# A hybrid RWKV/MoE step on one core: expert weights in six 2 MB units, gather by a stationary selection, biases in 32-row quadrants

## The chip, the core and the metric

One core of a Trainium2 chip runs the whole kernel in one launch. Times are device microseconds of that core. The engines are TensorE (PE, its weight loads are shown apart as PEld), VectorE (DVE), ScalarE (ACT), GpSimd (POOL) and SyncE (SP), which here only issues transfers. Transfers run on the core's 16 DMA engines. The metric is the time of one execution, as the median of several runs.

## The reference, cut to what matters

Two streams of 128 tokens (context and latent, D = 1024) go through one layer: modulation, norm, an input projection, a pooling and an RWKV branch, an output projection, and then a mixture of 32 experts, each token with the 4 experts that its router picks. The change touches the experts alone. All weights and activations are f32.

```python
def moe(h, lp):
    xt = h.reshape(B * T, D)
    logits = (xt @ lp['router_w'] + lp['router_b']).astype(jnp.float32)
    top_v, top_i = lax.top_k(logits, TOP_K)
    top_w = jax.nn.softmax(top_v, axis=-1)
    combine = jnp.sum(jax.nn.one_hot(top_i, N_EXPERTS, dtype=jnp.float32) * top_w[..., None], axis=1)
    for e in range(N_EXPERTS):
        gu = xt @ lp['expert_w_gu'][e] + lp['expert_b_gu'][e]
        glu = jnp.minimum(gu[:, :D_FF], SWIGLU_LIMIT)
        lin = jnp.clip(gu[:, D_FF:], -SWIGLU_LIMIT, SWIGLU_LIMIT)
        act = glu * jax.nn.sigmoid(SWIGLU_ALPHA * glu) * (lin + 1.0)
        out = out + combine[:, e:e + 1] * (act @ lp['expert_w_down'][e] + lp['expert_b_down'][e])
```

An expert's weights are 1024 x 2048 (gate and up, 8 MB) and 1024 x 1024 (down, 4 MB).

## The kernel before, in words

The first 390 us do everything up to the router. Then a loop runs over work items. An item is one expert with up to 64 of its tokens (SLOTS); an expert with more tokens gets further items. With these inputs there are 32 items. Every engine has its own loop over the items, and semaphores tie them together; the order within an engine is the order of the code.

**Weights.** `ring` holds 12 slots of 1 MB (128 partitions of 8 KB), one item's weights. SyncE (`expert_chunk`, L380 to L388, loop at L418) waits until `chunk_used` says that a slot has been read, and issues the same slot of the next item. Slots 0 to 7 hold gate and up, slot j the rows 128 j to 128 j + 127 (8 KB a partition, one run). Slots 8 to 11 hold down, two blocks of 128 rows each (two runs of 4 KB a partition).

**TensorE, one item** (L1185 to L1233). The stationary operand is always the small one, 64 slots wide, the moving operand is 512 columns of weights. Two output halves `h` go to the two 64-partition halves of a bank, so two 64-column tiles of the array work side by side. In turn:
- gate and up (L1192): 8 chunks by 4 matmuls into banks G (gate) and L (up). After chunk 1 the gate's bias is added (L1175, `up_bias(G, 0, False)`): the stationary `sele` has row e set to ones and picks row e of the bias table.
- `gather()` for the next item (L1147): 16 matmuls, x in 128-column blocks stationary, the 0/1 selection `p2` (64 columns) moving. It leaves the chosen tokens already transposed, hidden dimension on partitions; ScalarE copies them to `xg` (L1521).
- four transposes of the activation (L1203), two of the weighted selection (L1208).
- down (L1216): 4 chunks by 4 matmuls into G, with the down bias (L1222) after the first chunk.
- the up bias of the next item into L (L1175, `up_bias(L, FF, True)`).
- scatter (L1232): the result times the weighted selection, added into banks 0 to 3, in two row tiles of 64.

**VectorE, one item:** the weighted selection (L1973), the next selection (L1903), then after gate and up: clip the gate (L1981), clip the up part (L1982), (up + 1) times gate (L1984), times the sigmoid (L1987), the copy of the transposed activation (L1989), and the next `sele` (L1907). **ScalarE:** the sigmoid with its table load (L1532), the copy of the gathered tokens (L1521), of the transposed selection (L1535), of the down result (L1538).

**GpSimd** fills the unused rows of the bias tables with zeros ahead of the loop and loads them.

## Time and profile before

| | us |
|---|---|
| median of 3 runs | 1373.55 |
| lowest, highest | 1370.78, 1376.55 |
| the profiled execution | 1377.59 |
| its span, first to last instruction | 1375.8 |
| TensorE busy | 1315.5 |
| VectorE busy | 342.0 |
| ScalarE busy | 201.3 |
| GpSimd busy | 34.5 |
| mean granted clock | 0.98 |

The profile is that of one execution. The span is 1.8 us shorter than the time of the same execution. "Granted clock" is the share of TensorE's full 2.4 GHz. "PEld" rows are the weight loads, which run ahead of the matmuls that they belong to; since their starts are recorded and the ends of matmuls are modelled, the prediction reads distances between starts of loads. An f32 matmul is recorded as two loads and two matmuls.

### The profile page before, as it was taken

How to read it: one execution, taken by the hardware profiler on the slowest of the kernel's cores; microseconds unless marked ns; L12 is line 12 of the kernel's file. 1: busy time of each engine (PE TensorE's matmuls, PEld its weight loads, DVE VectorE, ACT ScalarE, POOL GpSimd, SP SyncE). 2: the span in 40 equal slices, each digit the busy share in tenths (PEclk: the TensorE clock that was granted, in tenths of full speed). 3: DMA queues.
4: the chain of work that ended last, by engine and by line, in shares of the span. 5: the costliest groups of instructions: out<-in, count | busy, mean ns of one | idle time of the engine just before them, and what ended most of it. 6: DMA issues, size and time to landing. Idle time of an engine off the chain costs nothing.

```text
span 1375.8 us, 19277 instructions
## 1 busy us (share of the span) xinstructions
PE 1315.5 (96%) x7509; PEld 687.7 (50%) x7509; DVE 342.0 (25%) x756; ACT 201.3 (15%) x365; POOL 34.5 (3%) x72
## 2 busy tenths in 40 slices
PE   4999999999999999999999999999999999999996
PEld 2676789878744344444443444444344444444442
DVE  0558962304331111111111111111111112111113
ACT  2331123110221111111111111111111111111111
POOL 3000110010000000000000000000000000000000
PEclk8899999979999999999999999999999999999998
DMA  9968401247459999999999999999999999999990
GB/s 325 330 208 301 135 12 53 93 157 288 171 232 402 416 414 408 415 415 415 413 413 408 412 415 412 413 416 407 415 413 409 415 415 416 413 405 414 416 385 30
DMA packets 109388, 462.45 MB, mean 336 GB/s; under 512 B 10695, under 2 KB 33902, under 8 KB 76558
## 3 DMA queue, kind: packets, MB, share of 16 engines
q1 hardware_dynamic: 107134, 457.68, 84.1%
q0 software_dynamic: 848, 3.03, 0.6%
q10 hardware_dynamic: 1376, 1.31, 0.3%
q8 instruction: 22, 0.36, 0.1%
q14 instruction: 8, 0.07, 0.0%
HBM read 460.66 MB, written 1.33 MB: 336 GB/s over the span
## 4 chain that ended last, share of the span: by engine, by line
PE 92%; DVE 4%; DMA 2%; issue 1%; SPq 1%; ACT 0%; DVEq 0%
PE bank L1192 32%; PE bank L1216 16%; PE bank L1147 9%; PE bank L1232 4%; PE bank L1175 4%; PE bank L608 4%; PE bank L633 3%; PE bank L1044 2%; PE bank L1081 2%; PE bank L1222 2%; DMA ring<-in_w_mod 2%; DVE pmT L1989 2%; PE bank L1203 1%; PE bank L564 1%; PE bank L744 1%; PE bank L946 1%
## 5 line engine op out<-in xcount | busy, mean ns | idle before, releaser
L1192 PE MATMUL bank<-ring,gate 128*64 128x512 f32 x2048 | 451.9, 594 | 0.0
L1192 PEld LDWEIGHTS bank<-ring,gate 128*64 128x64 f32 x2048 | 144.3, 137 | 298.2 <-issue 298.1
L1216 PE MATMUL bank<-ring,pmT 128*64 128x512 f32 x1024 | 232.4, 595 | 20.5 <-DVE pmT L1989 20.5
L1981 DVE TENSOR_SCALAR gate<-bank 128x512 f32<-128x512 f32 x32 | 22.1, 692 | 563.5 <-PE bank L1192 563.5
L1216 PEld LDWEIGHTS bank<-ring,pmT 128*64 128x64 f32 x1024 | 73.1, 137 | 153.6 <-issue 153.6
L1147 PEld LDWEIGHTS bank<-vt,bt 128*128 128x128 f32 x1024 | 116.7, 192 | 26.0 <-issue 26.0
L1147 PE MATMUL bank<-vt,bt 128*128 128x64 f32 x1024 | 121.1, 276 | 0.0
L1532 ACT ACTIVATE corr<-gate 128x512 f32<-128x512 f32 x32 | 20.1, 630 | 521.6 <-DVE gate L1981 521.6
L1175 PE MATMUL bank<-qr,vt 128*64 128x512 f32 x260 | 67.0, 592 | 0.0
L1232 PE MATMUL bank<-kk 64*128 64x512 f32 x256 | 63.6, 615 | 0.0
L633 PE MATMUL bank<-hnT,ring 128*128 128x256 f32 x240 | 56.6, 392 | 2.9 <-issue 2.9
L1538 ACT ACTIVATE kk<-bank 128x512 f32<-128x512 f32 x32 | 19.1, 597 | 262.6 <-PE bank L1216 262.6
L608 PE MATMUL bank<-hnT,ring 128*128 128x256 f32 x256 | 55.9, 379 | 0.0
L633 PEld LDWEIGHTS bank<-hnT,ring 128*128 128x128 f32 x240 | 45.8, 195 | 14.0 <-issue 7.9
L608 PEld LDWEIGHTS bank<-hnT,ring 128*128 128x128 f32 x256 | 48.5, 190 | 6.5
L1907 DVE COPY vt<-ident 128x64 f32 (+1 forms) x33 | 6.5, 196 | 152.7 <-PE bank L1216 152.7
L1232 PEld LDWEIGHTS bank<-kk 64*128 64x128 f32 x256 | 22.0, 186 | 41.0 <-issue 41.0
L1532 ACT ACT_TABLE_LOAD x32 | 41.1, 1283 | 1.9 <-DVE tick L1964 1.3
L1175 PEld LDWEIGHTS bank<-qr,vt 128*64 128x64 f32 x260 | 18.9, 137 | 37.0 <-issue 37.0
L564 PE MATMUL bank<-ring,cpad 128*32 128x256 f32 x384 | 29.5, 441 | 7.8 <-DMA ring<-in_w_mod 7.8
L1989 DVE COPY pmT<-bank 128x512 f32<-128x512 f32 x32 | 22.1, 692 | 45.1 <-PE bank L1203 45.1
L1222 PE MATMUL bank<-qr,vt 128*64 128x512 f32 x128 | 33.1, 592 | 0.0
(352 smaller groups left out, 975.4 us busy)
## 6 DMA issues: line engine op xcount, KB each, us to landing
ring<-in_expert_w_gu SPq DMA_DIRECT2D x256, 1024.0 KB, 8.6
ring<-in_expert_w_down SPq DMA_DIRECT2D x128, 1024.0 KB, 7.6
ring<-in_w_mod SPq DMA_DIRECT2D x24, 1024.0 KB, 10.4
ring<-in_w_in SPq DMA_DIRECT2D x17, 1024.0 KB, 8.1
ring<-in_w_o SPq DMA_DIRECT2D x4, 1024.0 KB, 9.7
ring<-in_w_pool_out SPq DMA_DIRECT2D x2, 1024.0 KB, 7.0
ring<-in_w_rwkv_out SPq DMA_DIRECT2D x2, 1024.0 KB, 11.8
pr<-gate_rows POOLq DMA_DIRECT2D x4, 512.0 KB, 7.3
```

What stands on the lines that cost most here:

```text
L564: last = mm(out[32 * j:32 * (j + 1), :], cpad[:, 2 * r + k, :], w[:, k, j * MW:(j + 1) * MW], start=(r + k == 0), stop=(r == MC - 1 and k ...
L608: last = mm(o, ring_in(c)[:, k, (m % 2) * P:(m % 2 + 1) * P], hnT[:, k, :], start=(k == 0), stop=(k == KT - 1))
L633: last = mm(banks[n % 2][:, 0:TT], w[:, k, o:o + P], hnT[:, k, :], start=(i == 0), stop=(i == KT - 1))
L1044: last = mm(banks[m % 4][:, 0:TT], ring_in(c)[:, k, (m % 4) * P:(m % 4 + 1) * P], src[:, k, :], start=(k == 0), stop=(k == 3))
L1147: last = mm(banks[6][:, k * SLOTS:(k + 1) * SLOTS], x2t[:, s, k * P:(k + 1) * P], p2[:, s, 0:SLOTS], start=(s == 0), stop=(s == NS - 1))
L1175: mm(b[h * SLOTS:(h + 1) * SLOTS, :], sele, bgu[:, o + h * 512:o + (h + 1) * 512], start=start, stop=False)
L1192: last = mm(b[h * SLOTS:(h + 1) * SLOTS, :], xg[:, j, :], ring[:, j, o + h * 512:o + (h + 1) * 512], start=(j == 0 and b is G), stop=(j == ...
L1216: last = mm(G[h * SLOTS:(h + 1) * SLOTS, :], actT[:, c % 4, c // 4, :], ring[:, GU_CHUNKS + j, i * D + h * 512:i * D + (h + 1) * 512], sta ...
L1222: mm(G[h * SLOTS:(h + 1) * SLOTS, :], sele, bdn[:, h * 512:(h + 1) * 512], start=False, stop=False)
L1232: last = mm(banks[2 * s + h][:, :], pwt[r, s, :], ysb[r, :], start=False, stop=True, skip_group_check=True)
L1532: af(sgb, gsb, ACT.Sigmoid, scale=ALPHA).then_inc(S("sg_ready"), 1)
L1989: v.tensor_copy(actT.rearrange("p j h s -> p (j h s)"), banks[5][:, :]).then_inc(S("actT_ready"), 1)
```

## The change

- **Weights:** six units of 2 MB instead of twelve of 1 MB. A unit takes two neighbouring slots. Partition p gets the rows 2p and 2p + 1 of a block of 256 (gate and up), or rows 4p to 4p + 3 of a block of 512 (down), one run of 16 KB. The first item's units are issued a little later, when two slots are free at once.
- **Gather:** the selection is stationary (64 columns), x is moving (512 columns): 4 matmuls, in the middle of gate and up, with the tokens on partitions. ScalarE copies the result to `xgt`, TensorE turns it in four transposes with a stride of 2 (`gather_turn`), and ScalarE copies that to `xg`.
- **Activation transposes:** they read `act_[:, i::4]`, a stride of 4, to match the new order of the down rows.
- **Biases:** the table of 2048 gate-and-up biases is laid out as four groups of 32 partitions (one for each 512 columns), the down table as two groups. `sele` has row e of every quadrant set (`quad`), and each bias matmul reads 32 rows. All four gate and up biases come after scatter, the two down biases after the gate has been evicted and ahead of the activation's transposes. GpSimd no longer fills the tables.

```diff
-    bgu = area[:, 0:2048]
-    bdn = area[:, 2048:3072]
+    bgu = area[:, 0:512]
+    bdn = area[0:2 * NE, 512:1024]
...
+        def expert_unit(e, u):
+
+            if u < GU_UNITS:
+                src = A["expert_w_gu"][0][bass.ds(e, 1), 2 * P * u:2 * P * (u + 1), :].rearrange("o (p i) n -> p (o i n)", i=2)
             else:
...
+                r = 4 * P * (u - GU_UNITS)
+                src = A["expert_w_down"][0][bass.ds(e, 1), r:r + 4 * P, :].rearrange("o (p i) n -> p (o i n)", i=4)
+            sp.dma_start(ring[:, 2 * u:2 * u + 2, :].rearrange("p g n -> p (g n)"), src).then_inc(S(f"slot{2 * u}_full"), 16)
...
         def gather():
-            for k in range(KT):
-                for s in range(NS):
-                    last = mm(banks[6][:, k * SLOTS:(k + 1) * SLOTS], x2t[:, s, k * P:(k + 1) * P], p2[:, s, 0:SLOTS],
+
+            for s in range(NS):
+                for h in range(2):
+                    last = mm(banks[6][h * SLOTS:(h + 1) * SLOTS, :], p2[:, s, 0:SLOTS], x2t[:, s, h * 512:(h + 1) * 512],
                               start=(s == 0), stop=(s == NS - 1))
             last.then_inc(S("gathered"), 1)
+
+        def gather_turn():
+
+            for jj in range(2):
+                for i in range(2):
+                    c = 2 * jj + i
+                    last = tr(banks[6][:, c * P:(c + 1) * P], xgt[:, 2 * P * jj + i:2 * P * (jj + 1):2], ident[:])
+            last.then_inc(S("xgT_done"), 1)
...
+        def up_bias():
+
+            for b, r in ((G, 0), (L, 2)):
+                for h in range(2):
+                    q = slice((r + h) * NE, (r + h + 1) * NE)
+                    mm(b[h * SLOTS:(h + 1) * SLOTS, :], sele[q, :], bgu[q, :], start=True, stop=False)
...
+                if u == 1:
+                    pe.wait_ge(S("sel_ready"), it + 2)
+                    gather()
+
+            pe.wait_ge(S("xgt_ready"), it + 2)
+            gather_turn()
             pe.wait_ge(S("pw_ready"), it + 1)
...
+            pe.wait_ge(S("g_ready"), it + 1)
+            for h in range(2):
+                q = slice(h * NE, (h + 1) * NE)
+                last = mm(G[h * SLOTS:(h + 1) * SLOTS, :], sele[q, :], bdn[q, :], start=True, stop=False)
+            last.then_inc(S("sele_used"), 1)
+
+            pe.wait_ge(S("act_ready"), it + 1)
+            for i in range(4):
+                last = tr(L[:, i * P:(i + 1) * P], act_[:, i::4], ident[:])
+            last.then_inc(S("actT_done"), 1)
...
+            pe.wait_ge(S("sele_ready"), it + 2)
+            up_bias()
```

TensorE in the loop of the kernel before, from the last gate-and-up chunk to the first down chunk; `pmT` is the activation, `vt` the selections, `qr` the bias tables:

```order
L1192 MATMUL bank<-ring,gate 64x512 [waits slot7_full]
L1198 REGISTER_ALU
L1147 MATMUL bank<-vt,bt 128x64 [waits sel_ready]
L1147 MATMUL bank<-vt,bt 128x64 x15
L1203 MATMUL bank<-ident,pmT 128x128 [waits act_ready]
L1203 MATMUL bank<-ident,pmT 128x128 x3
L1208 MATMUL bank<-ident,vt 128x128 [waits pw_ready]
L1212 REGISTER_ALU [waits actT_ready]
L1216 MATMUL bank<-ring,pmT 64x512 [waits slot8_full]
```

The same place after the change; `raw` holds the gathered tokens ahead of their transposes:

```order
L1200 MATMUL bank<-ring,gate 64x512 [waits slot6_full]
L1200 MATMUL bank<-ring,gate 64x512 x7
L1155 MATMUL bank<-ident,raw 128x128 [waits xgt_ready]
L1155 MATMUL bank<-ident,raw 128x128 x3
L1211 MATMUL bank<-ident,vt 128x128 [waits pw_ready]
L1217 MATMUL bank<-qr,vt 64x512 [waits g_ready]
L1222 MATMUL bank<-ident,pmT 128x128 [waits act_ready]
L1222 MATMUL bank<-ident,pmT 128x128 x3
L1228 REGISTER_ALU [waits actT_ready]
L1232 MATMUL bank<-ring,pmT 64x512 [waits slot8_full]
```

The 16 gather matmuls are gone from here; four transposes and the down bias stand ahead of the activation's transposes.

TensorE at the end of an item, before:

```order
L1216 MATMUL bank<-ring,pmT 64x512 [waits slot11_full]
L1216 MATMUL bank<-ring,pmT 64x512 x3
L1175 MATMUL bank<-qr,vt 64x512 [waits sele_ready]
L1175 MATMUL bank<-qr,vt 64x512
L1232 MATMUL bank<-kk 128x512 [waits ysb_ready,pwt_ready]
L1232 MATMUL bank<-kk 128x512 x3
```

And after:

```order
L1232 MATMUL bank<-ring,pmT 64x512 [waits slot10_full]
L1232 MATMUL bank<-ring,pmT 64x512 x7
L1241 MATMUL bank<-kk 128x512 [waits ysb_ready,pwt_ready]
L1241 MATMUL bank<-kk 128x512 x3
L1183 MATMUL bank<-qr,vt 64x512 [waits sele_ready]
L1183 MATMUL bank<-qr,vt 64x512 x3
```

The bias matmuls moved from ahead of scatter to behind it, and are four instead of two.

## Rows read from the trace of the kernel before

**Rows 1.** The page, busy time by engine, and the chain that ended last
```profile
PE 1315.5 (96%) x7509; PEld 687.7 (50%) x7509; DVE 342.0 (25%) x756; ACT 201.3 (15%) x365; POOL 34.5 (3%) x72
...
PE 92%; DVE 4%; DMA 2%; issue 1%; SPq 1%; ACT 0%; DVEq 0%
```

**Rows 2.** Stretches of one item, then the last item whole: busy us, granted clock, DMA
```profile
core 0: us, PE busy (x) PEld busy (x) DVE busy (x) ACT busy (x) POOL busy (x), PEclk, DMA share, GB/s
907.88:922.62 14.74, 14.74 (x71) 4.79 (x69) 0.00 (x0) 0.00 (x0) 0.00 (x0) 1.00 1.02 420
922.62:927.70 5.08, 4.45 (x40) 4.21 (x38) 3.37 (x5) 1.61 (x3) 0.00 (x0) 1.00 1.00 418
927.70:936.44 8.74, 8.73 (x40) 2.88 (x40) 1.28 (x5) 0.72 (x2) 0.00 (x0) 1.00 1.01 412
936.44:938.36 1.92, 1.92 (x10) 0.69 (x9) 0.00 (x0) 1.16 (x1) 0.00 (x0) 1.00 1.01 382
...
1334.65:1365.13 30.48, 29.84 (x156) 12.56 (x154) 4.21 (x8) 2.21 (x4) 0.00 (x0) 1.00 0.15 60
```

**Rows 3.** The page, costliest groups: busy us, mean ns, the bias matmuls
```profile
L1175 PE MATMUL bank<-qr,vt 128*64 128x512 f32 x260 | 67.0, 592 | 0.0
```

**Rows 4.** Timeline of the same item: start us, us, engine, line, [idle before]
```profile
908.36 0.14 PEld L1192 LDWEIGHTS bank<-ring,gate 128*64 128x64 f32 x2 [0.28 <-issue]
...
921.66 0.14 PEld L1192 LDWEIGHTS bank<-ring,gate 128*64 128x64 f32 x2 [0.28 <-issue]
922.62 3.65 PEld L1147 LDWEIGHTS bank<-vt,bt 128*128 128x128 f32 x32 [0.81 <-issue]
...
922.74 0.69 DVE L1981 TENSOR_SCALAR gate<-bank 128x512 f32<-128x512 f32 x1 [17.79 <-PE bank L1192]
...
923.46 0.63 ACT L1532 ACTIVATE corr<-gate 128x512 f32<-128x512 f32 x1 [16.35 <-DVE gate L1981]
...
924.79 0.69 DVE L1987 TENSOR_TENSOR pmT<-corr 128x512 f32<-128x512 f32 x1
926.13 0.48 PEld L1203 LDWEIGHTS bank<-ident,pmT 128*128 128x128 f32 x4
...
927.70 0.20 PEld L1216 LDWEIGHTS bank<-ring,pmT 128*64 128x64 f32 x4 [0.87 <-issue]
```

**Rows 5.** Timeline, the end of the same item and the next one's start
```profile
934.62 0.15 PEld L1216 LDWEIGHTS bank<-ring,pmT 128*64 128x64 f32 x2 [0.28 <-issue]
...
935.70 0.60 ACT L1538 ACTIVATE kk<-bank 128x512 f32<-128x512 f32 x1 [8.21 <-PE bank L1216]
936.31 1.28 ACT L1532 ACT_TABLE_LOAD   x1
936.44 0.30 PEld L1232 LDWEIGHTS bank<-kk 64*128 64x128 f32 x4 [0.81 <-issue]
...
938.36 0.20 PEld L1192 LDWEIGHTS bank<-ring,gate 128*64 128x64 f32 x4 [0.76 <-issue]
```

**Rows 6.** Timeline early on: modulation matmuls in four 32-column tiles, and what follows
```profile
58.65 0.59 PEld L564 LDWEIGHTS bank<-ring,cpad 128*32 128x32 f32 x16 [0.76 <-issue]
...
59.65 0.51 PEld L633 LDWEIGHTS bank<-hnT,ring 128*128 128x128 f32 x3 [0.41 <-issue]
```

**Rows 7.** Issues of one item (timeline), landing of the first and the eighth (by line)
```profile
910.00 13.20 SPq L388 DMA_DIRECT2D ring<-in_expert_w_gu  x8
...
DMA to landing us min/median/max: 6.5/6.5/6.5
...
DMA to landing us min/median/max: 11.1/11.1/11.1
```

**Rows 8.** Stretches around two falls of the granted clock, columns as in rows 2
```profile
265.20:268.50 3.30, 3.30 (x22) 2.50 (x18) 2.54 (x5) 0.00 (x0) 0.00 (x0) 1.00 1.05 406
268.60:285.50 16.90, 16.90 (x59) 14.07 (x59) 0.00 (x0) 1.32 (x4) 0.00 (x0) 0.50 0.26 96
43.30:46.50 3.20, 3.20 (x9) 2.52 (x8) 1.59 (x3) 0.00 (x0) 0.00 (x0) 0.50 1.06 378
```

More of the change, by code:

```diff
@@ L419, in _ @@
             e = sp.value_load(item[0:1, bass.ds(it, 1)], min_val=0, max_val=NE - 1)
[L420 to L423 removed]
+            for u in range(NU):
+                sp.wait_ge(S("chunk_used"), it * NU + (u + 1 - NU))
+                expert_unit(e, u)
         sp.wait_ge(S("stored"), 96)
@@ L1159, in _ @@
         pe.wait_ge(S("sel_ready"), 1)
-        for k in range(KT):
-            for s in range(NS):
-                last = mm(banks[6 + k // 4][:, (k % 4) * P:(k % 4 + 1) * P], x2t[:, s, k * P:(k + 1) * P], p2[:, s, :],
-                          start=(s == 0), stop=(s == NS - 1))
-        last.then_inc(S("gathered"), 1)
+        gather()
         pe.wait_ge(S("e16_ready"), 1)
@@ L1180, in _ @@
+        pe.wait_ge(S("bgu_in"), 64)
+        pe.wait_ge(S("bdn_in"), 32)
         pe.wait_ge(S("sele_ready"), 1)
-        up_bias(L, FF, True)
         pe.wait_ge(S("items_ready"), 1)
         n_items = pe.value_load(item[0:1, ITEMS:ITEMS + 1], min_val=NE, max_val=NE + EXTRA)
+        up_bias()
         with pe.Fori(0, n_items) as it:
             pe.wait_ge(S("xg_ready"), it + 1)
-            for j in range(GU_CHUNKS):
-                pe.wait_ge(S(f"slot{j}_full"), it * 16 + 16 * (FRONT_USES[j] + 1))
-                for b, o in ((G, 0), (L, FF)):
-                    for h in range(2):
-                        last = mm(b[h * SLOTS:(h + 1) * SLOTS, :], xg[:, j, :], ring[:, j, o + h * 512:o + (h + 1) * 512],
-                                  start=(j == 0 and b is G), stop=(j == GU_CHUNKS - 1))
-                last.then_inc(S("chunk_used"), 1)
-                if j == 1:
-                    up_bias(G, 0, False)
-            pe.wait_ge(S("sel_ready"), it + 2)
-            gather()
-            pe.wait_ge(S("act_ready"), it + 1)
-            for j in range(4):
-                last = tr(L[:, j * P:(j + 1) * P], act_[:, j * P:(j + 1) * P], ident[:])
-            last.then_inc(S("actT_done"), 1)
@@ new lines, in _ @@
+            for u in range(GU_UNITS):
+                pe.wait_ge(S(f"slot{2 * u}_full"), it * 16 + 16 * (FRONT_USES[2 * u] + 1))
+                w = ring[:, 2 * u:2 * u + 2, :]
+                for i in range(2):
+                    for b, o in ((G, 0), (L, FF)):
+                        for h in range(2):
+                            last = mm(b[h * SLOTS:(h + 1) * SLOTS, :], xg[:, 2 * (u % 2) + i, u // 2, :], w[:, i, o + h * 512:o + (h + 1) * 512],
+                                      start=False, stop=(u == GU_UNITS - 1 and i == 1))
+                last.then_inc(S("chunk_used"), 1)
+                if u == 1:
+                    pe.wait_ge(S("sel_ready"), it + 2)
+                    gather()
@@ L1520, in gathered_out, with gather_turn_out @@
             act.wait_ge(S("gathered"), n)
-            af(xg.rearrange("p k s -> p (k s)"), banks[6][:, :], ACT.Copy).then_inc(S("xg_ready"), 1)
-        act.wait_ge(S("gathered"), 1)
-        for j in range(2):
-            last = af(xg[:, 4 * j:4 * j + 4, :], banks[6 + j][:].rearrange("p (k s) -> p k s", k=4)[:, :, 0:SLOTS], ACT.Copy)
-        last.then_inc(S("xg_ready"), 1)
+            af(xgt, banks[6][:, :], ACT.Copy).then_inc(S("xgt_ready"), 1)
+        def gather_turn_out(n):
+            act.wait_ge(S("xgT_done"), n)
+            af(xg.rearrange("p k h s -> p (k h s)"), banks[6][:, :], ACT.Copy).then_inc(S("xg_ready"), 1)
+        gathered_out(1)
+        gather_turn_out(1)
         act.wait_ge(S("items_ready"), 1)
```

92 lines of the change are left out of this document (39 added, 53 removed).

## The prediction

> **What bounds the kernel now.** The shares of the span and the chain of work come first [rows 1]: TensorE is busy for 96% and holds 92% of the chain, transfers 2%. The reader should then ask what TensorE waits for, and read the table by stretches for one expert (an item) [rows 2]. An item takes 30.48 us: 14.74 gate and up, 5.08 until the down weights start, 8.74 down, 1.92 scatter. The granted clock is 1.00 in all four stretches, so the full 2.4 GHz.
>
> The same rows show a second resource that is full: the 16 DMA engines' share is 1.00 to 1.02, at 382 to 420 GB/s. Which of the two sets the pace? The last item, the last of these rows, has nearly no transfers beside it (share 0.15) and also takes 30.48. And of the eight gate-and-up issues of an item the first, at 910.0, landed after 6.5 us and the last, at 922.9 (910.00 + 13.20 less its own 0.33), after 11.1 [rows 7], where a slot is used again a round of 30.48 after its last use, so some 28 us after the issue. Their landings are (922.9 + 11.1 - 910.0 - 6.5) / 7 = 2.50 us apart, so 12 MB need 30.0 us. TensorE sets the pace, with the transfers 1 to 2% behind. Larger units can thus give nothing by themselves; what decides is how TensorE's own item changes.
>
> **The unit of the sum.** Within a stretch the weight loads come in pairs (two 64-column tiles side by side, each row of the view is a pair), 31 intervals from 908.36 to 921.66 [rows 4]: 0.429 us a step. Every f32 matmul is two instructions, so a pair of 512-column matmuls takes two steps. Scatter has 4 steps and takes 1.92 [rows 5], so a change of tiling costs about 0.20 on top.
>
> **Part by part, per item.**
> 1. Gate and up. Today 34 steps: 32 for the weights, 2 for the gate bias. The bias leaves (-2), the new gather with the selection stationary comes in between units 1 and 2: 4 matmuls of 512 columns, 64-column tiles in pairs, 4 steps. No tiling changes. +0.86.
> 2. From the last up matmul to the first down load, 5.08 today. The old gather (32 instructions) holds TensorE from 922.62 to 926.13, 3.51; the activation chain on VectorE is done before that, at 924.79 + 0.69 = 925.48 [rows 4], 2.86 into the stretch. With the gather gone, the chain ends last. What TensorE does meanwhile is hidden: six transposes of 0.11 each (the four loads of L1203 take 0.48 with a last one of 0.14), 0.7 us together, then the down bias, which waits for the gate's eviction (922.74 + 0.69, 0.81 in) and takes two steps and a change of tiling, so it is over near 2.0. The activation's transposes start at 2.86 + 0.06 for the hand-over, then the same 1.57 (926.13 to 927.70) as today. 4.49, -0.59. On ScalarE the copy of the gathered rows and a second table load (1.28 us [rows 5]) come ahead of the sigmoid, in its wait of 16.35 us for the gate [rows 4]; the copy of the turned rows comes behind it, beside VectorE's three remaining operations. They cost nothing while that wait stays above some 2 us.
> 3. Down. The two bias steps inside go: -0.86. The up bias at its end (two steps, half of L1175's 8 instructions per item [rows 3]) lay in the wait for ScalarE's copy of the result: last down load 934.62, copy 935.70 to 936.30, scatter 936.44 [rows 5]. Taking it out frees at most the 0.14 behind the copy; I take 0.05. -0.91.
> 4. After scatter comes a new, exposed piece: all four up biases, 32 rows by 64 columns each, in four quadrants. If the four run at once: 2 steps and a change of tiling, 0.86 + 0.20. The nearest row for four at once is L564, 16 instructions of 256 columns from 58.65 to 59.65 [rows 6]: 4 steps of 0.215 and 0.14. Bounds 0.9 (if the change of tiling is 0.04) and 1.92 (only two at once, as scatter); I take 1.04, near L564. Behind it waits the next item's first weight matmul, and nothing covers it.
>
> Sum: +0.86 - 0.59 - 0.91 + 1.04 = +0.40 us an item, 30.9. The last item's bias is behind its scatter and ends nothing: 31 x 0.40 - 0.64 = +11.8. Ahead of the loop the first gather shrinks, but it then needs a copy, transposes and a copy, beside VectorE's list of items; the four biases come after the register load. I put that at 0, give or take 1. GpSimd's dropped fills, its bias transfers in six parts instead of two, and VectorE's one new reduction early on lie beside longer work of TensorE, and the first experts' units are issued during the output projection, over 15 us ahead of their use; these go at nothing.
>
> **The clock.** It fell to 0.50 after 265.2 to 268.5, though TensorE shows busy for all 3.30 us [rows 8]; these are pairs of 64-column matmuls with a change of tiling after each, so few columns flow. It held in today's 5.08 [rows 2]. The new 4.5 us stretch is emptier: 0.7 of transposes, 0.9 of bias, about 0.9 of waiting, 0.45 of transposes, 1.1 of waiting. It lies between these rows. A short fall costs about half of 3.2 us (the stretch from 43.3 to 46.5) [rows 8], 1.6. I count two falls in 32 items, +3.2, and keep none and ten for the range.
>
> **Transfers.** An item of 30.9 leaves them 0.9 us of room. With 2 MB units a slot comes free later, but each still has over 20 us until its use. SyncE issues 6 per item instead of 12 and has nothing else in its queue in the loop.
>
> Forecast: +11.8 + 3.2 = +15.0. The profiled execution took 1377.59 (span 1375.8 and 1.8 around it) and would become 1392.6; it is 4 above the median of the runs, 1373.55, so the predicted median is 1388.6, rounded to 1389.
>
> **What the Trainium skill says.** L564's row shows four tiles at once at nearly full gain. The page "TensorE: Matmul & The Clock Gate", Part 3, gives a measured 3.07x for four 32-row tiles at 512 columns; by it the quadrants' 0.86 would be 1.12, and the time 8 us more. The page on SBUF ("SBUF — State Buffer", the note on cachelines) says that reads which cross to a new 16-byte line each time pay a penalty, and names 4 fp32 as the limit of a free stride; the activation's new transposes read with a stride of 4 floats, those of the gather with 2. No row here has such a read. That rule is rival B.
>
> **Rivals.**
> A. Only two quadrant tiles at once: the biases cost 1.92, +0.88 x 31 = +27, and 1373.6 + 11.8 + 27 = 1413, with no falls of the clock since the new stretch is filled longer. For it: scatter with its two row tiles runs in pairs. Against: L564's four.
> B. Strided reads slow the four exposed transposes. Doubled, 4 x 0.11 = 0.44 an item: +14: 1403. For the gather's transposes it would be hidden.
> C. The clock falls in ten items, not two: +16 instead of +3: 1401. It is decided by how the emptier stretch counts, which only the new clock rows can show.
> D. The transfers become the bound. They start to hold TensorE when 12 MB take over 31.5 us (31 rounds of 30.9, and some 18 us of slack that the full ring gives), 2.62 per MB against 2.50. At 2.72: 31 x 32.6 - 31 x 30.9 - 18 = +35: 1424. Nothing here shows 16 KB runs, but 8 KB and 4 KB runs land alike.
> E. Faster: the quadrant biases slip into the drain of the scatter and cost nothing exposed. 31 x (0.40 - 1.04) = -20: 1353. It decides below 0.64. Against: scatter is itself followed by a gap before the next load (0.76 idle behind L1232 [rows 5]).
> F. No measurable change: several terms each a tenth smaller, the clock holding: +5: 1379.
>
> **How the numbers follow.** Forecast 47% (1381 to 1396), A 12%, B 12%, C 13%, D 3%, E 4%, F 9%. The range 1379 to 1414 takes in the forecast, A, B, C and F's upper edge, some 83%. A measurement of this kernel can tell 0.5%, 6.9 us, from no change. Faster by more is E, 4%; within it F and a sliver of the forecast, 10%; slower 86%.
>
> **What would show it.** Right: the item is 30.8 to 31.0; gate and up 15.6; the stretch after it 4.5 with a wait on VectorE's product before the activation's transposes; scatter start to next item 2.9 to 3.0; the DMA share drops below 1.0. Wrong: the quadrant matmuls start in pairs 0.43 apart (A); the activation's transposes are spaced 0.2 (B); the mean granted clock of the loop falls below 0.99 (C); TensorE waits for a slot (D); the next item's first load follows the scatter by under 0.6 (E).

## The result and the profile after

| | before | after |
|---|---|---|
| median of the runs, us | 1373.8 | 1394.9 |
| lowest, highest | 1370.8, 1376.6 | 1393.7, 1395.4 |
| the profiled execution | 1377.59 | 1394.64 |
| its span | 1375.8 | 1392.9 |
| first gate-and-up load of the loop | 389.54 | 386.68 |
| one item (start of gate and up to the next) | 30.48 | 30.93, four of them 32.62 |

The ratio is 1.0153, 95% interval 1.0130 to 1.0175: slower by 21 us, where 15 were forecast. From the start of the loop to the end of the span it is 986.3 us before and 1006.2 after, +19.9. That sum closes: without the falls the 31 items are 13.7 longer (0.44 each), four falls of the clock by 1.70 are 6.8, and the last item with what follows is 0.5 shorter, as it has no bias behind it.

The page of the changed kernel: busy time, the chain that ended last, and from the costliest groups those in which TensorE now waits and the new bias matmuls. Columns as in [rows 1] and [rows 3].

```profile
PE 1268.3 (91%) x6853; PEld 596.7 (43%) x6853; DVE 340.8 (24%) x757; ACT 254.9 (18%) x429; POOL 31.1 (2%) x74
...
PE 84%; DVE 10%; ACT 2%; DMA 2%; issue 2%; SPq 1%; DVEq 0%
...
L1232 PE MATMUL bank<-ring,pmT 128*64 128x512 f32 x1024 | 233.6, 610 | 27.5 <-DVE pmT L2006 27.5
...
L1241 PE MATMUL bank<-kk 64*128 64x512 f32 x256 | 63.6, 611 | 25.1 <-ACT kk L1554 25.1
...
L1222 PE MATMUL bank<-ident,pmT 128*128 128x128 f32 x128 | 23.9, 310 | 30.3 <-DVE pmT L2004 30.3
...
L1183 PE MATMUL bank<-qr,vt 32*64 32x512 f32 x264 | 35.9, 613 | 0.8 <-issue 0.8
```

In the profiled executions TensorE is busy for 47 us less and the kernel takes 17 us longer: work was taken out of places where it filled a wait, and put where nothing covers it. VectorE's part of the chain rose from 4% [rows 1] to 10%. TensorE now stands still at three places in each item: 0.95 us for VectorE's product ahead of the activation's transposes, 0.86 for its copy of them, 0.78 for ScalarE's copy of the down result. Before, it stood still at one of them, 0.64 for the copy of the transposes, as the waits of the kernel before show (engine, line, what it waited for: us in total, times, longest):

```profile
PE bank L1216 <- DVE pmT L1989: 20.5, 32, 0.6
```

The table by stretches of one item (915.86 to 946.78), to be read against [rows 2], then the 850 us in the middle of the loop:

```profile
core 0: us, PE busy (x) PEld busy (x) DVE busy (x) ACT busy (x) POOL busy (x), PEclk, DMA share, GB/s
915.86:931.46 15.60, 15.60 (x77) 5.08 (x73) 0.00 (x0) 1.88 (x2) 0.00 (x0) 1.00 0.98 400
931.46:935.98 4.52, 2.71 (x17) 1.48 (x15) 3.47 (x6) 1.39 (x3) 0.00 (x0) 1.00 1.01 431
935.98:943.82 7.84, 7.08 (x32) 2.28 (x33) 1.08 (x4) 0.70 (x2) 0.00 (x0) 1.00 1.00 405
943.82:946.78 2.96, 2.93 (x16) 0.98 (x16) 0.00 (x0) 1.19 (x1) 0.00 (x0) 1.00 1.01 426
...
450.00:1300.00 850.00, 780.06 (x3668) 269.83 (x3666) 122.85 (x270) 140.93 (x191) 0.00 (x0) 0.99 0.99 404
```

Gate and up +0.86, the stretch ahead of down -0.56, down -0.90, scatter and biases +1.04. In the two long stretches the transfers moved 420 and 412 GB/s before [rows 2] and move 400 and 405 here, and their share stays at 0.98 to 1.00: it doesn't show that they are the limit.

The timeline around the two new places, to be read against [rows 4] and [rows 5]:

```profile
933.62 0.69 DVE L2004 TENSOR_TENSOR pmT<-corr 128x512 f32<-128x512 f32 x1
934.37 0.56 PEld L1222 LDWEIGHTS bank<-ident,pmT 128*128 128x128 f32 x4 [1.83 <-DVE pmT L2004]
...
935.97 0.20 PEld L1232 LDWEIGHTS bank<-ring,pmT 128*64 128x64 f32 x4 [1.05 <-issue]
...
943.82 0.33 PEld L1241 LDWEIGHTS bank<-kk 64*128 64x128 f32 x4 [1.64 <-issue]
...
945.76 0.21 PEld L1183 LDWEIGHTS bank<-qr,vt 32*64 32x64 f32 x8 [0.76 <-issue]
...
946.78 0.65 PE L1200 MATMUL bank<-ring,gate 128*64 128x512 f32 x2
```

VectorE's product ends at 934.31, and the transposes' loads begin at 934.37: the activation chain ends last, as forecast. The eight loads of the four bias matmuls stand within 0.21 us, and the next weight matmul follows 1.02 after the first of them: two pairs, one after the other, would need four steps of 0.43, so all four quadrants ran at once.

### The profile page after: what moved, and what is told of

Same layout as the page of the kernel before. It is cut to its first block, busy times and chain, and to the rows that moved or that the text cites. A ratio compares the mean times of both kernels' runs of the same rounds, so it can differ in the third digit from the quotient of the medians.

```text
span 1392.9 us, 17218 instructions
## 1 busy us (share of the span) xinstructions
PE 1268.3 (91%) x6853; PEld 596.7 (43%) x6853; DVE 340.8 (24%) x757; ACT 254.9 (18%) x429; POOL 31.1 (2%) x74
## 4 chain that ended last, share of the span: by engine, by line
PE 84%; DVE 10%; ACT 2%; DMA 2%; issue 2%; SPq 1%; DVEq 0%
PE bank L1200 32%; PE bank L1232 17%; PE bank L1241 5%; PE bank L606 4%; PE bank L1146 4%; PE bank L631 3%; PE bank L1183 2%; PE bank L1042 2%; PE bank L1079 2%; PE bank L1222 2%; DVE corr L2001 2%; DVE pmT L2006 2%; DVE pmT L2004 2%; DMA ring<-in_w_mod 2%; DVE gate L1998 2%
## 5 line engine op out<-in xcount | busy, mean ns | idle before, releaser
L1533 ACT ACTIVATE raw<-bank 128x512 f32<-128x512 f32 x33 | 19.7, 597 | 340.8 <-PE bank L1146 340.8
L1146 PE MATMUL bank<-bt,vt 128*64 128x512 f32 x264 | 62.3, 592 | 0.0
L1241 PEld LDWEIGHTS bank<-kk 64*128 64x128 f32 x256 | 24.8, 186 | 65.6 <-issue 65.6
L1222 PE MATMUL bank<-ident,pmT 128*128 128x128 f32 x128 | 23.9, 310 | 30.3 <-DVE pmT L2004 30.3
L1222 PEld LDWEIGHTS bank<-ident,pmT 128*128 128x128 f32 x128 | 17.9, 209 | 58.5 <-DVE pmT L2004 58.5
L1183 PE MATMUL bank<-qr,vt 32*64 32x512 f32 x264 | 35.9, 613 | 0.8 <-issue 0.8
L1146 PEld LDWEIGHTS bank<-bt,vt 128*64 128x64 f32 x264 | 18.9, 137 | 37.1 <-issue 37.1
```

Of the source, the lines that this page charges most:

```text
L1146: last = mm(banks[6][h * SLOTS:(h + 1) * SLOTS, :], p2[:, s, 0:SLOTS], x2t[:, s, h * 512:(h + 1) * 512], start=(s == 0), stop=(s == NS - 1))
L1183: mm(b[h * SLOTS:(h + 1) * SLOTS, :], sele[q, :], bgu[q, :], start=True, stop=False)
L1222: last = tr(L[:, i * P:(i + 1) * P], act_[:, i::4], ident[:])
L1241: last = mm(banks[2 * s + h][:, :], pwt[r, s, :], ysb[r, :], start=False, stop=True, skip_group_check=True)
L1533: af(xgt, banks[6][:, :], ACT.Copy).then_inc(S("xgt_ready"), 1)
```

## The experiments

All ran on the chip, with the kernel before beside them (medians 1372.5 to 1374.0). "Item" is the distance from one item's first gate-and-up load to the next's. Items and falls of the clock are those of the one profiled execution of each kernel; e6_gather_blocks and e7_plain_turns ran once, and their time is that one execution's.

### One part at a time

**e1_units: the kernel before with the 2 MB units alone.**

```diff
-            for j in range(RING):
-                sp.wait_ge(S("chunk_used"), it * RING + (j + 1 - RING))
-                expert_chunk(e, j)
+            for u in range(NU):
+                sp.wait_ge(S("chunk_used"), it * NU + (u + 1 - NU))
+                expert_unit(e, u)
...
-                    last = mm(banks[6][:, k * SLOTS:(k + 1) * SLOTS], x2t[:, s, k * P:(k + 1) * P], p2[:, s, 0:SLOTS],
+                        last = mm(banks[6][:, k * SLOTS:(k + 1) * SLOTS], x2t[:, s, 2 * P * u + i:2 * P * (u + 1):2], p2[:, s, 0:SLOTS],
...
-                last = tr(L[:, j * P:(j + 1) * P], act_[:, j * P:(j + 1) * P], ident[:])
+                last = tr(L[:, i * P:(i + 1) * P], act_[:, i::4], ident[:])
```

> The kernel before with the 2 MB units alone: six issues per item, 16 KB runs, x read with a stride of 2 by the old gather, the activation's transposes with a stride of 4; old gather, old bias tables and old places. Main theory (units are free, TensorE's own item decides): item 30.48 us as before, gate and up 14.74, the stretch after it 5.08, no falls of the clock in the loop, 1371 to 1377 us, ratio 1.000. Rival U (the 2 MB units carry the loss): the whole difference of 17 to 21 us shows here, 1390 or more, with waits for a slot. Rival S (strided reads): 16 strided stationary loads and 4 strided transposes lengthen the 5.08 to over 5.3, and the time to over 1381.

Measured: 1381.1 us, ratio 1.0049 (1.0031 to 1.0066). Item 30.75, no fall of the clock in the loop, no wait for a slot. The main theory missed: the units aren't free. Rival S holds. The timeline of e1_units, weight loads behind gate and up:

```profile
922.64 3.85 PEld L1147 LDWEIGHTS bank<-vt,bt 128*128 128x128 f32 x32 [0.81 <-issue]
926.35 0.60 PEld L1198 LDWEIGHTS bank<-ident,pmT 128*128 128x128 f32 x4
926.86 0.26 PEld L1203 LDWEIGHTS bank<-ident,vt 128*128 128x128 f32 x2
927.99 0.20 PEld L1213 LDWEIGHTS bank<-ring,pmT 128*64 128x64 f32 x4 [0.87 <-issue]
```

From the first gather load to the first transpose it is 3.71 us against 3.51 in [rows 4], and the whole stretch takes 5.35 against 5.08.

**e6_gather_blocks: e1_units with x in blocks of neighbouring columns.**

```diff
-                        last = mm(banks[6][:, k * SLOTS:(k + 1) * SLOTS], x2t[:, s, 2 * P * u + i:2 * P * (u + 1):2], p2[:, s, 0:SLOTS],
+                        last = mm(banks[6][:, k * SLOTS:(k + 1) * SLOTS], x2t[:, s, k * P:(k + 1) * P], p2[:, s, 0:SLOTS],
```

> The kernel before with the 2 MB units alone, as e1_units, but x read by the old gather in blocks of 128 neighbouring columns; the weights' rows then meet the wrong hidden rows, so this computes something else. e1_units had an item of 30.75 against 30.48, its 32 gather loads spread over 3.71 us against 3.51 and the transposes' four over 0.51 against 0.45. Theory (the stride of the reads is all that the units cost): 0.20 comes back, item 30.54 to 30.56. Rival (the larger transfers disturb TensorE's reads): 30.75.

Measured: 1374.9 in one run, item 30.55, and in its timeline 3.51 us again from the gather to the transposes:

```profile
918.85 3.65 PEld L1147 LDWEIGHTS bank<-vt,bt 128*128 128x128 f32 x32 [0.81 <-issue]
922.36 0.59 PEld L1198 LDWEIGHTS bank<-ident,pmT 128*128 128x128 f32 x4
```

So the transfers themselves cost TensorE nothing. The row order of the larger unit does, where it makes a stationary load read with a stride: 0.20 us for 32 loads with a stride of two floats, 0.07 for the four loads with a stride of four.

**e2_old_gather: the changed kernel with the old gather.**

```diff
-                if u == 1:
-                    pe.wait_ge(S("sel_ready"), it + 2)
-                    gather()
-
-            pe.wait_ge(S("xgt_ready"), it + 2)
-            gather_turn()
+            pe.wait_ge(S("sel_ready"), it + 2)
+            gather()
```

> The changed kernel with the old gather: x stationary, 16 matmuls of 64 columns behind gate and up, no turn of the gathered rows; the order behind it is activation transposes, selection transposes, down bias. Main theory: gate and up 13.88, then 5.08 plus up to 0.4 since the down bias (0.9 to 1.06) is longer than the rest of the wait for the activation's copy, down 7.84, scatter and biases 2.96: item 30.0 to 30.2, and no falls of the clock (3.5 us of matmuls stand in that stretch): 1358 to 1366 us. The transfers, 2.50 us per MB, then end at 30.0 and may set it. Rival (the new gather is not what costs, the quadrant biases are): item 30.9 and more, 1388 or more.

Measured: 1368.7, ratio 0.9956 (0.9941 to 0.9972), item 30.34, no fall in the loop. Gate and up 13.89, the next stretch 5.65, down 7.85, scatter and biases 2.96. The item is 0.14 over the upper end of the expectation, for which the stride's price in the gather, 0.20, is enough (not known when it was written): from the first gather load to the first transpose it is 3.70 here. The time is 3 us over its upper end. This is faster than both kernels: with the new gather taken out, the changed kernel gains. The rival (the exposed quadrant biases cost) is out.

**e3_old_bias: the changed kernel with the old biases.**

```diff
+                if u == 0:
+                    up_bias(G, 0, False)
...
-            for h in range(2):
-                q = slice(h * NE, (h + 1) * NE)
-                last = mm(G[h * SLOTS:(h + 1) * SLOTS, :], sele[q, :], bdn[q, :], start=True, stop=False)
-            last.then_inc(S("sele_used"), 1)
...
+                    if u == 0 and i == 1:
+                        for h in range(2):
+                            last = mm(G[h * SLOTS:(h + 1) * SLOTS, :], sele, bdn[:, h * 512:(h + 1) * 512], start=False, stop=False)
...
+            up_bias(L, FF, True)
             pe.wait_ge(S("pwt_ready"), it + 1)
             pe.wait_ge(S("ysb_ready"), it + 1)
...
-            up_bias()
```

> The changed kernel with the old biases: full-height tables, the gate's bias between units 0 and 1, the down bias inside down, the up bias ahead of scatter; the gather is the new one. Main theory: gate and up 16.46, the next stretch 4.5, down 8.7, scatter 1.92: item 31.6, +0.67 against the changed kernel, 1415 us with its four falls of the clock. With the down bias gone from the stretch ahead of down, that stretch is emptier still: if it is its emptiness that makes the clock fall, there are more than four falls of 1.7 us, up to one in nearly each item, 1415 to 1455. Rival (falls come from something else, as the transfers): four or fewer, 1408 to 1416. Rival for the biases (the exposed quadrants cost more than they save): below 1395.

Measured: 1444.0, ratio 1.0504. An undisturbed item takes 31.64, +0.71 against the changed kernel, as expected. 18 of 31 items have a fall of the clock. One of them, from the item's start to the fall, and the 3.4 us behind it (columns as in the table above); then TensorE's timeline ahead of that fall:

```profile
452.76:474.40 21.64, 18.83 (x92) 7.01 (x92) 3.37 (x5) 3.27 (x5) 0.00 (x0) 1.00 0.99 411
474.40:477.80 3.40, 3.40 (x10) 1.01 (x8) 0.00 (x0) 0.00 (x0) 0.00 (x0) 0.50 1.00 424
```

```profile
469.81 0.38 PE L1211 MATMUL bank<-ident,vt 128*128 128x128 f32 x2
472.14 0.75 PE L1216 MATMUL bank<-ident,pmT 128*128 128x128 f32 x4 [1.95 <-DVE pmT L2001]
473.75 3.06 PE L1226 MATMUL bank<-ring,pmT 128*64 128x512 f32 x8 [0.86 <-DVE pmT L2003]
```

Ahead of the fall TensorE had waited 1.95 and 0.86 us with four transposes between. With the down bias out of this stretch the falls went from 4 items to 18: that speaks for the emptiness of this stretch and against the transfers (their share is 0.99 here too); e10_both_fillers tests it from the other side.

The four corners, item in us without falls (2 MB units in all):

| | old biases | new biases |
|---|---|---|
| old gather | 30.75 | 30.34 |
| new gather | 31.64 | 30.93 |

The new biases gain 0.41 or 0.71, the new gather costs 0.89 or 0.59, and only the two kernels with it have falls in the loop. So the item's way from 30.48 to 30.93 is +0.27 for the units, +0.59 for the gather and -0.41 for the biases, added in the order units, biases, gather.

### The falls of the clock

**e4_filler: one more matmul in the wait for VectorE's product.**

```diff
             pe.wait_ge(S("g_ready"), it + 1)
+            mm(G[:, 0:256], ident[:], xgt[:, 0:256], start=True, stop=True)
             for h in range(2):
```

> The changed kernel with one more matmul (the identity stationary, 256 columns of the gathered rows moving, into the gate's bank ahead of the down bias, which overwrites it), in VectorE's stretch where TensorE waits. It adds 0.43 us of work that ends at about 2.4 of 2.9 us. Main theory: item 30.93 unchanged, the four falls of the clock in the loop vanish, 4 x 1.7 = 6.8 us less, 1388. Rival: the falls have nothing to do with how full this stretch is: 1395, falls as many. Second rival: the work is not hidden: +0.4 x 31 = 13 more.

Measured: 1392.6, item 30.93, three falls instead of four. Hidden it was, but it didn't do what was expected. The falls stand just behind the stretch (685.0, with the first down load at 684.5), so the next run puts the matmul later.

**e5_filler_late: the same matmul behind the activation's transposes.**

```diff
             last.then_inc(S("actT_done"), 1)
 
+            pe.wait_ge(S("xg_ready"), it + 2)
+            mm(banks[6][:, 0:256], ident[:], xgt[:, 0:256], start=True, stop=True)
+
             pe.wait_ge(S("actT_ready"), it + 1)
```

> The changed kernel with one more matmul of 256 columns (0.43 us), this time behind the activation's transposes, in the wait of 1.1 us for VectorE's copy of them. With the same matmul ahead of the down bias three falls of the clock in the loop were left of four, each just behind this place (685.0, 934.1, 1183.3, where the activation's transposes and the wait are over at 684.5). Theory: it is the part from the activation's transposes to the first down loads that is too empty: no fall in the loop, item 30.93, 1388 us. Rival: work anywhere in the stretch does not matter, three or four falls stay: 1393 to 1395. Second rival: it delays the first down load: +0.1 to 0.4 an item, 3 to 12 us more.

Measured: 1392.1, item 30.93, three falls again. The theory that the late part alone decides fell. Three against four says little by itself: e7_plain_turns below, with no filling at all, has two. A stretch of e5_filler_late ahead of a fall and the 3.5 us behind it; TensorE is busy for 5.1 of 6.5 us, and yet the clock goes to half:

```profile
710.00:716.50 6.50, 5.13 (x28) 2.30 (x26) 3.46 (x6) 1.39 (x3) 0.00 (x0) 1.00 1.03 441
716.50:720.00 3.50, 3.50 (x10) 1.00 (x8) 1.09 (x4) 0.00 (x0) 0.00 (x0) 0.51 1.00 426
```

**e10_both_fillers: both places, the second with 384 columns.**

```diff
             pe.wait_ge(S("g_ready"), it + 1)
+            mm(G[:, 0:256], ident[:], xgt[:, 0:256], start=True, stop=True)
...
+            pe.wait_ge(S("xg_ready"), it + 2)
+            mm(banks[6][:, 0:384], ident[:], xgt[:, 0:384], start=True, stop=True)
```

> The changed kernel with extra matmuls at both places: 256 columns ahead of the down bias (0.43 us) and 384 columns behind the activation's transposes (0.64 us, in the wait of 1.1). Either place alone left three falls of four. Theory (the stretch between the last up and the first down load is too empty as a whole, and a fall comes when enough of the emptiness falls together): no fall in the loop, item 30.93, 1386 to 1389 us. Rival (the falls come from something that a fuller stretch does not change): three or four falls, 1391 to 1395. Second rival: the work delays the first down load: +0.1 to 0.3 an item, 3 to 9 us more.

Measured: 1387.7, ratio 1.0103 (1.0086 to 1.0120), all 31 items at 30.93, no fall. The middle of the loop, with the row of the changed kernel above at 0.99:

```profile
450.00:1300.00 850.00, 813.77 (x3798) 284.31 (x3796) 122.77 (x270) 140.87 (x191) 0.00 (x0) 1.00 1.00 407
```

7.1 us less than the changed kernel, for four falls of 1.70. More work for TensorE, less time. That the emptiness of the stretch brings the falls is shown from both sides: emptier, 18 items with a fall; filled at both places, none. Filling one place leaves three. How full the stretch has to be is not shown.

### The strided transposes

**e7_plain_turns: the changed kernel, both sets of transposes on neighbouring columns.**

```diff
-                    last = tr(banks[6][:, c * P:(c + 1) * P], xgt[:, 2 * P * jj + i:2 * P * (jj + 1):2], ident[:])
+                    last = tr(banks[6][:, c * P:(c + 1) * P], xgt[:, c * P:(c + 1) * P], ident[:])
...
-                last = tr(L[:, i * P:(i + 1) * P], act_[:, i::4], ident[:])
+                last = tr(L[:, i * P:(i + 1) * P], act_[:, i * P:(i + 1) * P], ident[:])
```

> The changed kernel with both sets of transposes reading neighbouring columns (the gathered rows and the activation); the hidden rows then meet the wrong weights, so this computes something else. The four loads of the activation's transposes took 0.56 us against 0.48 before. Theory (a stride of 4 costs a little): the four back at 0.48, item 30.85 to 30.88, 2 us less. Rival (the 0.05 by which the item missed the forecast lies elsewhere): item 30.93.

Measured: one run of 1387.0, with two falls; item 30.83, 0.10 less. From the lines of 500 to 1300 us, the activation's transposes: first this kernel, then the changed one.

```profile
L1222 PEld LDWEIGHTS bank<-ident,pmT 128*128 128x128 f32 x100 | 10.4, 140 | 46.4 <-DVE pmT L2004 46.4
```

```profile
L1222 PEld LDWEIGHTS bank<-ident,pmT 128*128 128x128 f32 x100 | 14.0, 209 | 45.7 <-DVE pmT L2004 45.7
```

A load with a stride of four floats takes 209 ns against 140; from the first of these loads to the first down load it is 1.51 us here and 1.60 in the changed kernel. That is the whole 0.10 of the item, 3 us in all; the gathered rows' transposes, made plain too, give nothing, as they lie in a wait.

### Where the room is, and what the transfers allow

**e8_packed_units: old gather and quadrant biases, each in a wait.** The gather is split around the activation's transposes, the selection's transposes go into the gate's bank, and the down result into bank 7, so that the gate's and up's banks are free when ScalarE copies the result. The four biases then run in that wait.

```diff
             pe.wait_ge(S("sel_ready"), it + 2)
-            gather()
+            gather(0)
             pe.wait_ge(S("act_ready"), it + 1)
...
             last.then_inc(S("actT_done"), 1)
 
+            gather(1)
             pe.wait_ge(S("pw_ready"), it + 1)
...
-                last = tr(banks[7][:, s * T:(s + 1) * T], pw[:, s, :], ident[:])
+                last = tr(G[:, s * T:(s + 1) * T], pw[:, s, :], ident[:])
...
-                        last = mm(G[h * SLOTS:(h + 1) * SLOTS, :], actT[:, i, u, :], w[:, i, h * 512:(h + 1) * 512],
+                        last = mm(banks[7][h * SLOTS:(h + 1) * SLOTS, :], actT[:, i, u, :], w[:, i, h * 512:(h + 1) * 512],
...
             pe.wait_ge(S("pwt_ready"), it + 1)
+            pe.wait_ge(S("sele_ready"), it + 2)
+            up_bias()
+
             pe.wait_ge(S("ysb_ready"), it + 1)
```

> The old gather (strided x) split around the activation's transposes, 12 matmuls ahead and 4 behind; selection transposes into the gate's bank; down result and down bias in the bank 7, so that gate's and up's banks are free early and all four quadrant biases run in the wait for ScalarE's copy of the result; 2 MB units. TensorE's own item by the rows of the run with the old gather: 30.34 - 1.04 for the biases + 0.2 to 0.3 of change of tiling = 29.5. Main theory: the transfers then set the pace (2.50 us per MB in the profile of before): item 30.0 to 30.1, TensorE waits for slots, 1356 to 1361 us. Rival: transfers can go faster when they are asked to, item 29.5, 1343. Rival: 2 MB units are slower than 1 MB (landings at 404 GB/s): item 30.3 and more, no gain over 1368.7.

Measured: 1344.6, ratio 0.9790 (0.9773 to 0.9807), item 29.55 throughout. The rival that the transfers can go faster is right: no wait for a slot. The end of an item in its timeline:

```profile
944.56 0.21 PEld L1172 LDWEIGHTS bank<-qr,vt 32*64 32x64 f32 x8 [0.81 <-issue]
944.56 1.09 PE L1172 MATMUL bank<-qr,vt 32*64 32x512 f32 x8
944.68 0.60 ACT L1533 ACTIVATE kk<-bank 128x512 f32<-128x512 f32 x1 [7.38 <-PE bank L1218]
945.29 1.28 ACT L1527 ACT_TABLE_LOAD   x1
945.58 0.30 PEld L1230 LDWEIGHTS bank<-kk 64*128 64x128 f32 x4 [0.81 <-ACT kk L1533]
```

The biases run beside ScalarE's copy (944.68 to 945.28), and scatter begins at 945.58, 0.30 behind the copy. The piece of 1.04 us behind scatter has become 0.2: from the last down load to scatter it is 1.97 us, against 1.78 in e2_old_gather. Splitting the gather gives nothing: from gate and up to the first down load it is 5.71, against 5.64.

**e9_packed_chunks: the same order with twelve transfers of 1 MB and plain reads.**

```diff
-            for u in range(NU):
-                sp.wait_ge(S("chunk_used"), it * NU + (u + 1 - NU))
-                expert_unit(e, u)
+            for j in range(RING):
+                sp.wait_ge(S("chunk_used"), it * RING + (j + 1 - RING))
+                expert_chunk(e, j)
...
-                last = tr(L[:, i * P:(i + 1) * P], act_[:, i::4], ident[:])
+                last = tr(L[:, i * P:(i + 1) * P], act_[:, i * P:(i + 1) * P], ident[:])
```

> The same order of TensorE's work with the old 1 MB transfers, twelve per item, and plain x blocks and transposes. TensorE's own item: 29.5 - 0.27 = 29.2. Main theory (transfers set the pace, the size of a transfer does not matter): the same item as the run with 2 MB units within 0.05 us, 30.0 to 30.1, 1356 to 1361 us. Rival (size matters): the two differ by over 0.1 us an item. Rival (TensorE still sets it): this one is 0.27 an item faster, 1335 to 1350.

Measured: 1347.2, ratio 0.9810 (0.9790 to 0.9831). The item is 29.41 for 23 items, then 30.12: the ring's slack is used and TensorE waits for slots. The main theory, that the size of a transfer doesn't matter, missed. TensorE's own item is 0.14 under that of e8_packed_units, not 0.27: behind the split gather only the strided loads from the transposes on are exposed. The waits of e9_packed_chunks (engine, line, what it waited for: us in total, times, longest), and its middle in the table by stretches; below them the same row of e8_packed_units:

```profile
PE bank L1194 <- DMA ring<-in_expert_w_gu: 4.4, 9, 0.5
```

```profile
450.00:1300.00 850.00, 845.43 (x4428) 345.71 (x4426) 134.64 (x290) 96.21 (x143) 0.00 (x0) 1.00 1.02 418
```

```profile
450.00:1300.00 850.00, 850.00 (x4438) 355.26 (x4434) 134.62 (x290) 96.92 (x145) 0.00 (x0) 1.00 1.00 426
```

Its bound of 30.1 is what the forecast read from the landings before (2.50 us per MB, 30.0). The transfers in 2 MB units aren't held there: the form of the transfers matters, once TensorE asks for more. Size and run length (16 KB against 8 and 4 KB) changed together; which of them does it is not shown.

**e11_bias_once: e8_packed_units with the down bias as one product ahead of the loop.**

```diff
-            for h in range(2):
-                q = slice(h * NE, (h + 1) * NE)
-                last = mm(banks[7][h * SLOTS:(h + 1) * SLOTS, :], sele[q, :], bdn[q, :], start=True, stop=False)
...
+        pe.wait_ge(S("combT_ready"), 1)
+        for s in range(NS):
+            for h in range(2):
+                mm(banks[2 * s + h][:, :], combT[:, s * T:(s + 1) * T], bdn[:, h * 512:(h + 1) * 512], start=True, stop=True)
         with pe.Fori(0, n_items) as it:
```

> e8_packed_units without the down bias in the loop: its sum over a token's experts is one product of the combine weights and the bias table, and fills banks 0 to 3 once ahead of the loop in place of the zeros. TensorE's own item falls by the 1.17 us that change of tiling and down bias take there: 28.4. Ahead of the loop up to 3 us more. Theory (at 426 GB/s and a share of 1.00 the transfers are now full): item 29.3 to 29.5, TensorE waits for slots of the ring, 1336 to 1343 us. Rival (2 MB units have more room): item 28.4, no waits, 1308 to 1313. The 1 MB form was held at 30.1 an item (418 GB/s).

Measured: 1339.5, ratio 0.9760 (0.9743 to 0.9777). The item is 28.54 for 15 items behind a first of 31.0, then 29.36 to the end, with waits for slots: the theory, in its range. Its waits, then the stretches of the loop:

```profile
PE bank L1185 <- DMA ring<-in_expert_w_gu: 9.5, 16, 0.6
```

```profile
700.00:1000.00 300.00, 297.08 (x1567) 127.25 (x1568) 50.79 (x110) 35.32 (x53) 0.00 (x0) 1.00 1.01 429
1000.00:1300.00 300.00, 293.98 (x1534) 122.32 (x1532) 46.41 (x100) 35.69 (x52) 0.00 (x0) 1.00 1.01 429
```

12 MB in 29.36 us is 2.45 us per MB, and the item is 2.5% shorter than the 30.12 of the 1 MB form. That is what the change's units are worth where the transfers set the pace. Neither kernel of the pair could use it: TensorE's own item was longer than both limits.

The loop of e11_bias_once began at 397.8 instead of 386. Its front, by stretches:

```profile
370.00:380.00 10.00, 6.50 (x38) 4.70 (x36) 4.35 (x22) 4.30 (x8) 0.00 (x0) 0.77 0.10 41
380.00:390.00 10.00, 9.00 (x44) 7.47 (x43) 3.52 (x18) 1.87 (x2) 0.00 (x0) 0.50 0.00 0
390.00:400.00 10.00, 10.00 (x18) 3.26 (x16) 1.08 (x4) 0.01 (x1) 0.00 (x0) 0.50 0.01 2
```

**e12_bias_once_filled: e11_bias_once with the four matmuls of zeros kept.** They do nothing for the result.

```diff
+        pe.wait_ge(S("zero_ready"), 1)
+        zero_sums(0)
...
+        for j in (1, 2):
+            zero_sums(j)
...
+        zero_sums(3)
```

> e11_bias_once with the four 512-column matmuls of zeros kept at their old places ahead of the loop (the bias product overwrites what they write). In e11 the clock was at 0.50 from 375.5 for 27.3 us, from where the first of them had stood, and the loop began at 397.8 instead of 386. Theory (without them TensorE has too few columns there and the clock falls): no fall after the front's usual four, the loop begins at 388 to 390, first item 28.7 instead of 31.0, and since the transfers begin with the loop the whole end moves with it: 9 to 10 us less than e11, 1329 to 1332. Rival (the bias product or the transposes of the combine weights make it fall): 1337 to 1342 as e11. The transfers stay at 29.36 an item once the ring's slack is used.

Measured: 1333.5, ratio 0.9708 (0.9692 to 0.9724), 6 us less than e11_bias_once, 1.5 us past the slow end of what was expected. The long fall is gone, so leaving out the zeros had brought it. But the loop begins at 393.8, where 388 to 390 was expected, and behind the product (3.6 us, from 390.19) stands one fall of 3.4 us, at 394.4, in the first item, which takes 30.24. That the product brings this one is not shown. This is the fastest version: 40 us under the kernel before, 61 under the changed one.

## Why the prediction was right, and where it was not

**What bounds the kernel** was read rightly. TensorE's own item set the pace, and the 1 MB transfers were right behind it, at 30.1 (e9_packed_chunks) where 30.0 was forecast.

**Gate and up, +0.86:** measured 15.60, exactly that. **The stretch ahead of down, -0.59:** measured -0.56. The chain on VectorE ends last, the transposes start 2.91 us in (forecast 2.92). **Down, -0.91:** measured -0.90. **Scatter and biases, +1.04:** measured +1.04. The item was forecast at 30.88 and is 30.93.

The missing 0.05 is more than covered by the strided transposes (0.10 by e7_plain_turns), which the forecast had at zero and as rival B at 0.44. The forecast took over 1.57 us from the first transpose to the first down load; with plain reads it is 1.51, with the stride 1.60. So rival B's mechanism is there, at a quarter of its price. The forecast cited the Trainium skill ("SBUF — State Buffer", the note on cachelines): a read that goes to a new 16-byte line each time pays. The trace agrees in direction, 209 against 140 ns for a load. The same note names 4 fp32 as the limit of a free stride. Here the runs differ from it: the stride of four floats is not free, and e1_units against e6_gather_blocks shows that a stride of two already costs 0.20 us over 32 loads. This the prediction left out, since no exposed load of the changed kernel has that stride.

**The clock** is the term that was mis-sized: four falls of 1.70, +6.8, against two of 1.6, +3.2. The place and the size of a fall were right, the count a guess between none and ten. A fall of the changed kernel, then TensorE's timeline ahead of it:

```profile
562.20:565.60 3.40, 3.40 (x10) 1.00 (x8) 1.09 (x4) 0.00 (x0) 0.00 (x0) 0.51 1.04 443
```

```profile
557.81 1.07 PE L1217 MATMUL bank<-qr,vt 32*64 32x512 f32 x4
559.84 0.75 PE L1222 MATMUL bank<-ident,pmT 128*128 128x128 f32 x4 [0.95 <-DVE pmT L2004]
561.45 4.92 PE L1232 MATMUL bank<-ring,pmT 128*64 128x512 f32 x14 [0.86 <-DVE pmT L2006]
```

The same instructions stand in the 27 items without a fall. What differs is only when they come. The falls are not scattered: they begin at 562.2, 811.4, 1060.6 and 1340.5, so eight, eight and nine items apart, each 20.9 to 21.0 us into its item, some 0.8 behind the first down load; in e3_old_bias they come in every second item for long stretches. What picks the item is not shown. Reading one item doesn't give the count, and no row of the kernel before could tell four from two.

**The sum.** In the loop 15.0 were forecast and 19.9 measured: 1.3 more from the 31 items (13.7 against 31 x 0.40), 3.6 from the falls. Ahead of the loop the forecast had 0 give or take 1. The two profiled executions differ by -2.9 there, but nothing shows that as the change's: e1_units and e6_gather_blocks, with the old biases and the old gather, began their loops at 385.0 and 384.6. The clock was at half for 47.8 us ahead of the loop before and for 37.5 after. In the other variants up to e10_both_fillers that was 34.1 to 41.0 us, and their loops began between 384.6 and 388.0. The stretch from 260 to 300 us, before and then after:

```profile
260.00:300.00 40.00, 39.31 (x290) 33.11 (x288) 5.71 (x10) 3.81 (x10) 0.00 (x0) 0.74 0.36 124
```

```profile
260.00:300.00 40.00, 38.52 (x284) 31.75 (x281) 5.06 (x8) 3.87 (x11) 0.62 (x2) 0.79 0.45 152
```

It was right to add the sum to the profiled execution and then take off the 4 us by which that stood above its median: medians differ by 21.1 and loops by 19.9, the two profiled executions by 17.1 only. The last 1.2 stays open; it is within the spread of the runs.

**The rivals.** A (two quadrants at a time) is out: eight loads within 0.21 us and 1.02 to the next weight matmul. The Trainium skill ("TensorE: Matmul & The Clock Gate", Part 3) gives 3.07x for four 32-row tiles, by which, as an estimate, the two steps would be 1.12 and the piece 1.32; measured is 1.02 with the change of tiling in it. C (ten falls) is out; four lie between it and the forecast's two. D (the transfers become the bound) is out: there is no wait for a slot, and the rates in the long stretches were lower than before; the 2 MB units' own limit is 29.36 and left 1.6 us of room, not 0.9. E (the biases slip into scatter's drain) is out.

**"Larger units can thus give nothing by themselves"** held for the transfers and was wrong by omission: the units alone cost 0.27 us an item through the row order that they force on the reads (e1_units). In the changed kernel only the stride of four is exposed: the stride of two moved from the gather to the transposes of `gather_turn`, which lie in a wait.

## What to carry to other kernels

The new gather is cheaper by itself (four steps of 0.43 us against 3.51) and dearer in its place, since the old one filled a wait for VectorE and the new one stands among the weights: price a step by what ends last where it stands. Exposed pieces go into waits by freeing their banks (0.8 us an item in e8_packed_units for another bank under the down result), and only then does it matter what the transfers allow. Where a wait gets emptier, look at the granted clock of the next stretches, and be ready to fill it with work that does nothing.

## What the runs showed of the hardware that was not expected

- Four matmuls of 32 rows by 64 columns in four quadrants take 1.02 us with the change of tiling, against 1.72 for two full-height pairs (four steps of 0.429). Beside the two steps of one pair, 0.86, that leaves 0.16; scatter with its change of tiling has 0.20 on top of its steps.
- Stationary loads with a stride: 140 ns plain, 209 with a stride of four floats; 32 loads with a stride of two take 3.71 us against 3.51.
- One core's transfers reach 418 GB/s in 1 MB transfers with 8 KB and 4 KB runs, and 429 in 2 MB transfers with 16 KB runs, both at a share of 1.0. The Trainium skill ("DMA: Bandwidth & Descriptors", Where 436 GB/s comes from) names about 358 GB/s of HBM per core as what binds such loads; with one core at work these runs went well past it, towards its other figure, 435.
- Shares of 0.99 to 1.02 over 300 us and more stood beside 404, 418, 426 and 429 GB/s. It doesn't tell whether the transfers are the limit. A wait for a slot does.
- The clock fell with TensorE shown busy for 5.1 of the 6.5 us before. A matmul of 256 columns at either of two places left three falls of four; matmuls of 256 and 384 columns at both places left none. Without four matmuls of zeros ahead of the loop the clock was at 0.50 for 27 us there, and the kernel took 6.0 us longer (e11_bias_once against e12_bias_once_filled).
